# Later loading and multiplying of eight modulation slices between the first experts and the second mixer

## The reference, cut to what matters

```python
for l in range(DEPTH):
    mod_lat = jnp.split((sc @ w_ada[l] + b_ada[l])[:, None, :], 6, axis=-1)
    mod_ctx = jnp.split((scc @ w_ada[l] + b_ada[l])[None, None, :], 6, axis=-1)
    h_lat = modulate(rmsnorm(x_lat, g_mix[l]), mod_lat[0], mod_lat[1])
    ...                                  # even layer: mixer_ab; odd layer: mixer_c
    x_lat = x_lat + mod_lat[2] * y_lat
    h_lat = modulate(rmsnorm(x_lat, g_ffn[l]), mod_lat[3], mod_lat[4])
    ...                                  # moe over the tokens, added with mod[5]
```

## Time and profile before

| | |
|---|---|
| median of 3 runs (lowest, highest) | 2488.21 us (2487.07, 2488.29) |
| profiled execution: time, span | 2483.72 us, 2482.1 us |
| PE busy | 2314.4 us, 93% |
| DVE, ACT, POOL busy | 1623.8 us, 946.6 us, 388.4 us |
| chain that ended last | PE 75%, issue 10%, DMA 6%, DVE 4% |
| mean transfer rate | 262 GB/s |

### The profile page before, as it was taken

How to read it: one execution, slowest core, us unless ns; L and a number is a source line. 1 busy time by engine, 2 the same in 40 slices (tenths; PEclk the granted TensorE clock), 3 DMA queues, 4 the chain that set the end, 5 groups by cost and what they waited for, 6 DMA issues and landing times.

```text
span 2482.1 us, 42412 instructions
## 1 busy us (share of the span) xinstructions
PE 2314.4 (93%) x16299; PEld 1549.0 (62%) x16300; DVE 1623.8 (65%) x2006; ACT 946.6 (38%) x1167; POOL 388.4 (16%) x421
## 2 busy tenths in 40 slices
PE   6999989996999999999979999999999899999992
PEld 2555534544888888888857887666645455555541
DVE  2899985446988888888876651677534534344445
ACT  3000013114777777777754232466421111111111
POOL 0533432220000000000020001211000222122211
PEclk8999989997999999999989999999998999999996
DMA  9111085439999999999992133212534989999995
GB/s 337 59 44 59 34 309 160 167 131 374 422 422 402 391 389 381 389 387 390 351 349 76 59 128 114 70 56 77 206 133 178 387 352 380 405 418 421 420 420 227
DMA packets 154271, 649.95 MB, mean 262 GB/s; under 512 B 27818, under 2 KB 42570, under 8 KB 99410
## 3 DMA queue, kind: packets, MB, share of 16 engines
q1 hardware_dynamic: 126978, 579.11, 59.4%
q0 software_dynamic: 16336, 58.06, 6.6%
q10 hardware_dynamic: 10880, 11.74, 1.4%
HBM read 595.99 MB, written 52.86 MB: 261 GB/s over the span
## 4 chain that ended last, share of the span: by engine, by line
PE 75%; issue 10%; DMA 6%; DVE 4%; ACT 1%; POOL 1%; SPq 1%; POOLq 0%; ACTq 0%; DVEq 0%
PE ps L945 72%; DMA arena<-in_w_dram 3%; DMA xs_d<-arena 1%; DMA arena<-in_w_in_ab_dram 1%; PE ps L1143 1%; ACT arena L1565 1%; PE ps L1149 1%; PE ps L1165 1%; DVE arena L2300 1%; PE ps L1033 1%; DMA buf_d<-arena 0%; SPq L451 0%; DVE arena L2078 0%; POOL arena L764 0%; PE ps L1535 0%
## 5 line engine op out<-in xcount | busy, mean ns | idle before, releaser
L945 PE MATMUL ps<-arena 128*32 128x256 f32 (+4 forms) x10200 | 1174.6, 407 | 35.0 <-ACT arena L1565 15.2
L945 PEld LDWEIGHTS ps<-arena 128*32 128x32 f32 (+1 forms) x10200 | 642.3, 128 | 513.2 <-issue 317.1
L2346 DVE TENSOR_TENSOR wl<-wx,wh 128x2048 fp32r<-128x2048 f32 x228 | 511.7, 2286 | 27.4 <-ACT wh L1565 27.4
L1565 ACT ACTIVATE arena<-ps 128x256 f32<-128x256 f32 (+5 forms) x389 | 176.2, 478 | 871.4 <-PE ps L945 626.2
L1565 ACT ACTIVATE wh<-wx 128x2048 fp32r<-128x2048 f32 x228 | 432.4, 1915 | 86.1 <-PE ps L945 73.4
L2300 DVE COPY arena<-arena 128x2048 f32<-128x2048 f32 x180 | 211.1, 1237 | 279.0 <-PE ps L945 236.9
L945 PE MATMUL ps<-wh,xT 128*128 128x512 f32 x1216 | 388.6, 396 | 2.5 <-DVE xT L2363 2.5
L945 PEld LDWEIGHTS ps<-wh,xT 128*128 128x128 f32 x1216 | 229.4, 189 | 56.2 <-DVE xT L2363 3.1
L2397 DVE SCALAR_TENSOR_TENSOR arena<-arena,par 128x768 f32<-128x768 f32 x232 | 241.1, 1114 | 0.0
L945 PE MATMUL ps<-wl,xT 128*128 128x512 f32 x608 | 240.2, 395 | 0.0
L945 PE MATMUL ps<-wh,gT 128*128 128x512 f32 x608 | 199.5, 399 | 0.0
(11 more groups left out here) (355 smaller groups left out, 2266.9 us busy)
## 6 DMA issues: line engine op xcount, KB each, us to landing
wx<-in_w_dram SPq DMA_DIRECT2D x228, 1024.0 KB, 8.8
arena<-in_w_dram SPq DMA_DIRECT2D x192, 1024.0 KB
arena<-in_w_ada_dram SPq DMA_DIRECT2D x40, 1024.0 KB, 8.9
craw<-in_w_in_c_dram SPq DMA_DIRECT2D x8, 2048.0 KB, 8.7
buf_d<-arena POOLq DMA_DIRECT2D x1, 14848.0 KB, 57.5
arena<-buf_d POOLq DMA_DIRECT2D x20, 512.0 KB, 10.5
buf_d<-arena POOLq DMA_DIRECT2D x19, 512.0 KB, 8.0
arena<-in_w_in_ab_dram SPq DMA_DIRECT2D x8, 1024.0 KB, 12.6
```

The lines of the kernel that those rows point to most:

```text
L945: return pe.matmul(bank_ap, lhsT, rhs, start=first, stop=last)
L1565: return act.activation(out_, in_, f, **kw)
L2346: v.tensor_tensor(wl[:, g], wx[:, g], whs[g % NH].bitcast(F32), ALU.subtract).then_inc(m["low"], 1)
```

## The change

Items 20 to 23 are no longer loaded behind the experts. SP issues them in `chain(2)` when the x of tile 0 is ready, behind the `craw` load, which moves there from tile 2. Items 24 to 27 are loaded at the last tile, when `mods(20)` is done. On PE `mods` 20 and 21 stand behind the transposes of tile 2, 22 and 23 behind those of tile 3, and 24 to 27 behind column 0 of the mixer. The transposes of shift and scale go behind those of the last tile, since the scale is ready later. Vector 6 gets another PSUM bank (7), and column 3, which uses it too, waits for the copy. `vector_out(5)` and `vector_out(6)` and the wait for the `xs_d` stores on ACT move with them.

```diff
@@ SP, chain(2)
                     if n == 2 and i == 0:
                         sp.wait_ge(x_new, j + 1 - NT)
+                        sp.dma_start(craw, wc[:, :, 0:512]).then_inc(cw, 16)
+                        for k in range(20, 24):
+                            item_load(k)
+                    if n == 2 and i == NT - 1:
                         sp.wait_ge(u_mm, 21)
                         for k in range(24, 28):
                             item_load(k)
-                    if n == 2 and i == 2:
-                        sp.dma_start(craw, wc[:, :, 0:512]).then_inc(cw, 16)
@@ SP, behind the experts
-            for n in range(16, 24):
+            for n in range(16, 20):
                 sp.wait_ge(moe["used"], nb * PAIRS + (n - 16 + 4))
                 item_load(n)
@@ PE
-            for n in range(16, 24):
+            for n in range(16, 20):
                 mods(n)
             for t, j in tiles_of(2):
                 to_channels(2, t, j)
-                if t == 4:
-                    for n in range(24, 28):
+                if t in (2, 3):
+                    for n in range(16 + 2 * t, 18 + 2 * t):
                         mods(n)
-                if t == 2:
-                    pe.wait_ge(u_ev, 6)
-                    ...
+            pe.wait_ge(u_ev, 6)
+            ...
                 ins.then_inc(xm_mm, 1)
+                if ct == 0:
+                    for n in range(24, 28):
+                        mods(n)
+                if ct == 2:
+                    pe.wait_ge(u_ev, 7)
@@ ACT
-                    if n == 2 and t == 0:
+                    if n == 2 and t == NT - 1:
                         vector_out(5)
                 if n == 2:
                     act.wait_ge(cw, 16)
                     go(cw0h, craw[:, :, 0:P], ACT.Copy).then_inc(c_high, 1)
-                    vector_out(6)
                     turned(n, t, j)
...
-            await_stores(act, 3)
...
+            await_stores(act, 3)
             for ct in range(1, 4):
                 high_slice(ct)
+            vector_out(6)
             vector_store(6)
...
-VBANK = (0, 1, 2, 0, 0, 2, 0, 6, 0, 2)
+VBANK = (0, 1, 2, 0, 0, 2, 7, 6, 0, 2)
```

More of the change, by code:

```diff
@@ L1410, in _ @@
                 to_channels(2, t, j)
-                if t == 4:
-                    for n in range(24, 28):
+                if t in (2, 3):
+                    for n in range(16 + 2 * t, 18 + 2 * t):
                         mods(n)
-                if t == 2:
-                    pe.wait_ge(u_ev, 6)
[L1416 to L1420, removed]
+            pe.wait_ge(u_ev, 6)
+            for r in range(2):
+                for h in range(2):
+                    ins = pe.transpose(ps[:, 6, UW * r + P * h:UW * r + P * h + P],
+                                       vstage[4 + r][:, h * P:(h + 1) * P], ident)
+            ins.then_inc(a_mm, 1)
             for ct in range(KE):
```

## The result

The changed kernel takes 2495.09 us in the median of 9 runs (2490.57 to 2499.43), the kernel before beside it 2488.29 us (2485.73 to 2493.25). The ratio is 1.003, with a 95% interval of 1.002 to 1.004, that is 5 to 10 us slower. The profiled execution has a span of 2490.8 us against 2482.1.

What follows compares the result with a forecast made beforehand. PE was taken to bound the kernel, with no slack behind the seam. A modulation start 2.2 us later plus 4.1 us of matmuls behind column 0 made 6.3 us on 2488.2, so 2494.5 us, range 2486.5 to 2498.0.

Steps and rivals of the forecast that it cites:

- Term 1: Start of the tiles: the last expert store lands sooner, so x of tile 0 is complete 3.0 us earlier.
- Term 2: Behind tile 2: PE waits 7.5 us for items 20 to 23, landing 20.9 us after x; modulation starts 2.2 us later.
- The bound of no sharing at all: Landing of items 20 to 23: 18.1 us after x if no gather shared the transfer engines.
- The first pair of mods: `mods` 20 and 21 on PE, ahead of tile 3's transposes: 3.4 us at the lower clock.
- M: Time at which the modulation begins: 1310.56 before the change, forecast at 1312.8, 2.2 us later.
- Term 3: Behind column 0 of the mixer: `mods` 24 to 27 add 4.1 us on PE, with nothing hiding them.
- Rival (a): Items 20 to 23 land earlier, under 19.6 us after x, and it is a draw, loss under 5.0 us; chance 0.33.
- Rival (b): `mods` 24 to 27 are hidden behind column 0; with early items a gain of 5.3 us, chance 0.10.
- rival (c): Lower clock at tile 5 and late landings: 8.7 us loss, up to 2499 us if items 24 to 27 are late; beyond 2497, 0.07.

Runs made afterwards that it cites:

- The loads' return: Changed kernel with items 20 to 23 again loaded behind the experts, their matmuls still behind tiles 2 and 3: 2487.22 us beside 2487.53 of the kernel before, ratio 1.0002.
- the swap: Changed kernel with items 20 to 23 issued ahead of the first `craw` load instead of behind it: 2491.09 us beside 2487.53 of the kernel before, ratio 1.0017.
- alone: Kernel before, with only `mods` 24 to 27 moved behind column 0 and all loads where they were: 2486.29 us beside 2487.53, ratio 0.9999.
- doubled: Changed kernel with the matmuls of `mods` 24 to 27 done twice behind column 0: 2501.71 us beside 2488.05 of the kernel before, ratio 1.0061.
- the last version: Changed kernel, only items 22 and 23 held to tile 0, ahead of `craw`; `mods` 24 to 27 before column 0: 2479.83 us beside 2486.39 of before, ratio 0.9975.

## Why the prediction was right, step by step

The predicted 2494.5 us stand against 2495.09 measured: 6.3 us of loss predicted, 6.8 between the medians, 8.2 in the seam of the trace. The steps that carry it hold, and their sizes were off by 0.1 to 2.0 us. That the median came within 0.6 us is luck on top of it: the profiled execution was predicted at 2490.0 us and took 2492.41, and in the seam of both traces the loss was 8.2 and 8.5 us, 2 us more than the sum.

- **Term 1** held in its mechanism: without items 20 to 23 in the queue the store lands sooner. It lands in 5.12 us, not in the 3.9 of the lone store of the earlier trace rows, and the first gather takes 4.93 instead of 4.34. So the gather, and not DVE's second choices as I had it, was still what came last (0.57 us of wait), and x of tile 0 comes 2.4 us earlier, not 3.0. The loads' return (8.3 us again, x at 17.7) shows the cause.
- **Term 2**, the step on which all hung: the items landed 1302.1 - 1280.7 = 21.4 us after x; predicted 20.9. The 1.2 us that I took off for the gathers' lead were not there, since the gathers moved with x: the last one was issued 1.1 us after it, before the change 1.25. The `craw` share was 4.4 us and not 5.3: with the swap the items landed 17.0 us after x. These two errors, 1.2 us too little and 0.9 too much, cancel in part, which is why the sum is only 0.5 us off. PE waited 8.24 us instead of 7.5. The bound of no sharing at all, 18.1, was far off, and so was the estimate of 16.4 us from the Trainium skill ("DMA: Bandwidth & Descriptors", "Anatomy of one DMA"), which counts these transfers alone and no gathers beside them: measured 21.4 us for the transfers together.
- The first pair of mods was mis-sized, 3.4 us predicted and 1306.5 - 1302.15 = 4.4 measured. I had taken 4.06 / 56 from a row within which the clock rose; the 24 matmuls at the lower clock took 2.78 us instead of 1.74. From the turn of tile 3 to M it was 7.8 us, predicted 7.9, with the higher clock as chosen.
- Together M came 4.2 us later in the seam, not 2.2: about 0.6 us of the difference comes from term 1, 0.5 from the landing, 0.8 from the first pair with the transposes of tile 3.
- **Term 3**: predicted 4.1 us, measured 3.99, in the changed kernel, alone, and doubled. Items 24 to 27 were there in time: landed by 1318.7 us and used at 1330.70, a cover of 12 us where I had counted on 5.
- Rival (a) had the right lever, the arrival: with the items ahead of `craw`, or loaded early, the loss is 3.9 or 0.7 us of the seam. In the changed kernel they were late. Rival (b) is refuted by the doubled matmuls. Of rival (c), neither the lower clock at tile 5 nor late items 24 to 27 occurred in the changed kernel. The clock was a near thing: with the items ahead of `craw` it had fallen by then, at a price of 1.1 us, near the 1.2 of (c).

The measured ratio's interval reaches down to 5 us and up to 10 us; which of 6.8 and 8.2 us is nearer the truth the runs do not settle, as the rest of the kernel, from column 1 to the end, took 1156.1 us in one trace of the changed kernel and 1160.7 in the other.

## What to carry to other kernels

A load may be moved out of the way of an urgent transfer only if its consumer moves far enough with it: here the start won 2.4 us, and the consumer, though moved behind tile 2, waited 8.2 us on an engine that works in order. Add up the bytes ahead in the queue up to that consumer, and put what is used first in front. Work that is not urgent costs nothing only where the engine idles anyway; count that gap and whether the data are there, before placing it between two full columns.

## What the runs showed of the hardware

Two things that I had not expected. First, a 512 KB store moves its bytes fast and lands late. Windows of the changed kernel around its expert store (the last two columns are the share of the 16 engines and GB/s):

```profile
1268.00:1269.00 1.00, 1.00 (x24) 0.45 (x20) 0.97 (x2) 0.00 (x0) 0.03 (x1) 1.00 0.52 180
1269.00:1270.00 1.00, 0.62 (x12) 0.10 (x4) 0.96 (x2) 0.00 (x0) 0.00 (x0) 1.00 0.83 328
1270.00:1271.00 1.00, 0.00 (x0) 0.00 (x0) 1.00 (x1) 0.00 (x0) 0.00 (x0) 1.00 0.07 16
1271.00:1272.00 1.00, 0.00 (x0) 0.00 (x0) 0.96 (x2) 0.00 (x0) 0.00 (x0) 1.00 0.06 25
```

Nearly all bytes move in two microseconds; then the share of the 16 engines is 0.07 and 0.06, about one engine's worth, for another two, and `done` waits for the landing at 1272.57. Whether that is one slow engine or a little of several, the windows do not show. Second, SP's issue of the same four loads takes very different times. SP's queue with the items ahead of `craw`:

```profile
1281.37 1.94 SPq L463 DMA_DIRECT2D arena<-in_w_ada_dram  x4
```

SP's queue in the changed kernel, at its two groups of four item loads (the first behind `craw`, the second behind the four stores):

```profile
1281.16 5.78 SPq L463 DMA_DIRECT2D arena<-in_w_ada_dram  x4
...
1304.95 2.38 SPq L463 DMA_DIRECT2D arena<-in_w_ada_dram  x4
```

SP's queue in the last version, behind two items and `craw`:

```profile
1280.75 10.46 SPq L463 DMA_DIRECT2D arena<-in_w_ada_dram  x4
```

Four item loads took SP 1.94 us when they were first in the queue, 2.38 behind the four stores, 5.78 behind `craw`, and 10.46 behind two items and `craw`. My reading is that the issue takes longer the more is still outstanding; whether the bytes or the kind of the transfers ahead set it, no run separates. What stands behind in SP's stream starts later by it: the first store of x starts 7.1 us after its x is complete in the last version (1291.26), and 1.3 us after it in the changed kernel (1286.98).
